# Attention in place and one unit deeper, all turned copies on ScalarE, query blocks in the order 0, 3, 2, 1

## The reference

```python
# first block, "nsa": for each of 4 query blocks of 128 tokens and each of 4 heads
p_c = masked_softmax(q . k_cmp, ...)        # 31 compressed keys
p_s = masked_softmax(q_rope . k_sel, ...)   # keys up to the query
p_w = masked_softmax(q_rope . k_win, ...)   # keys up to the query
prob = softmax(q_mem . mem_k)               # 256 memory keys
# second block, "dsa": for each of 4 query blocks, 16 heads
rel = relu(einsum('bqhd,bsd->bhqs', qib, k_idx))        # 8 index heads
score = einsum('bqh,bhqs->bqs', wb, rel)                # causal
_, sel = lax.top_k(score, topk)                         # topk = 128
p = softmax(q . k at the selected, valid keys)
o = p @ v at the same keys
```

## Time and profile before

| | |
|---|---|
| three executions | 2140.89, 2128.39, 2145.9 us (median 2140.89) |
| profiled execution, device time | 2129.25 us |
| its span in the profile | 2127.3 us |
| `stage_nsa`, attention part | about 459 to 609 us |
| `stage_dsa`, index items | about 772 to 798.5 us |
| `stage_dsa`, attention part | about 798.5 to 966 us |
| `stage_dsa`, output turned and copied | about 967 to 972.4 us |

### The profile page before, as it was taken

The page is one execution under the profiler, slowest core; times in us unless marked ns, Lnnn a source line. Parts: engine busy times, 40 slices in busy tenths (PEclk is TensorE's granted clock), DMA queues, the critical chain, the costliest instruction groups (busy, mean ns, idle before and its releaser), DMA issues. The chain is left out here.

```text
span 2127.3 us, 31283 instructions
## 1 busy us (share of the span) xinstructions
PE 1922.6 (90%) x12332; PEld 1519.9 (71%) x12332; DVE 973.7 (46%) x1686; ACT 824.1 (39%) x1304; POOL 259.9 (12%) x209
## 2 busy tenths in 40 slices
PE   5999389879978889998799999989999889999997
PEld 4887189745547646667688888868888768888885
DVE  2343835473354588834333333345555443333233
ACT  4223244433223443323444442246565244344322
POOL 3000223110003150000200000022222030000000
PEclk9999579865569995558799999989999899999998
DMA  4321100000002110002122333322222113322331
GB/s 169 98 90 45 38 5 3 29 17 1 1 22 84 50 31 1 1 1 60 60 91 96 99 94 100 94 72 88 73 71 60 41 60 99 99 94 94 99 99 50
DMA packets 37762, 131.66 MB, mean 62 GB/s; under 512 B 4817, under 2 KB 5137, under 8 KB 37393
## 3 DMA queue, kind: packets, MB, share of 16 engines
q1 hardware_dynamic: 36784, 127.91, 19.0%
q10 hardware_dynamic: 864, 2.17, 0.3%
HBM read 127.17 MB, written 2.10 MB: 61 GB/s over the span
## 5 line engine op out<-in xcount | busy, mean ns | idle before, releaser
L138 DVE TENSOR_TENSOR big_parts<-ring,big_parts 128x1024 fp32r<-128x1024 f32 x164 | 205.1, 1252 | 526.8 <-ACT big_parts L133 526.8
L156 PE MATMUL bank<-h_parts,big_parts 128*128 128x512 f32 x960 | 381.9, 398 | 26.0 <-POOL y_parts L1402 17.6
L157 PE MATMUL bank<-y_parts,big_parts 128*128 128x512 f32 x960 | 377.8, 394 | 0.0
L158 PE MATMUL bank<-h_parts,big_parts 128*128 128x512 f32 x960 | 377.5, 393 | 0.0
L133 ACT ACTIVATE big_parts<-ring 128x1024 fp32r<-128x1024 f32 x164 | 173.7, 1061 | 289.2 <-PE bank L158 289.0
L156 PEld LDWEIGHTS bank<-h_parts,big_parts 128*128 128x128 f32 x960 | 182.9, 191 | 67.3 <-issue 28.3
L158 PEld LDWEIGHTS bank<-h_parts,big_parts 128*128 128x128 f32 x960 | 182.7, 190 | 38.5
L157 PEld LDWEIGHTS bank<-y_parts,big_parts 128*128 128x128 f32 x960 | 183.1, 191 | 37.3
L157 PE MATMUL bank<-y_parts,work_parts 128*128 128x512 f32 x456 | 181.4, 398 | 0.0
L138 DVE TENSOR_TENSOR work_parts<-ring,work_parts 128x1024 fp32r<-128x1024 f32 x65 | 79.3, 1223 | 168.0 <-ACT work_parts L133 168.0
L995 ACT ACTIVATE work<-work 128x256 f32<-128x256 f32 (+4 forms) x128 | 67.1, 525 | 209.7 <-DVE work L1013 209.6
(11 more groups left out here) (399 smaller groups left out, 3121.3 us busy)
## 6 DMA issues: line engine op xcount, KB each, us to landing
ring<-in_wstream SPq DMA_DIRECT2D x229, 512.0 KB, 3.5
x<-in_xt SPq DMA_DIRECT2D x4, 512.0 KB, 7.9
out_t<-x SPq DMA_DIRECT2D x8, 256.0 KB, 2.0
work<-in_memt ACTq DMA_DIRECT2D x1, 1024.0 KB, 15.4
work<-in_cw SPq DMA_DIRECT2D x1, 1024.0 KB, 5.1
cst<-in_cst ACTq DMA_DIRECT2D x1, 704.0 KB, 7.9
cos<-in_reset SPq DMA_DIRECT2D x2, 256.0 KB, 2.6
big<-work SPq DMA_DIRECT2D x4, 128.0 KB, 4.0
```

What stands on the lines that cost most here:

```text
L138: dve.tensor_tensor(self.parts[:, self.place_of(n), 1, :, :], self.ring[:, n % RING, :, :], self.parts[:, self.place_of(n), 0, :, :].bitca ...
L156: pe.matmul(out, w[0], x[0], start=start, stop=False, skip_group_check=True)
L157: pe.matmul(out, w[0], x[1], start=False, stop=False, skip_group_check=True)
L158: return pe.matmul(out, w[1], x[0], start=False, stop=stop, skip_group_check=True)
```

## The change

Four things change in `Attend` and one in `stage_dsa`. R writes its masked scores straight into the weights buffer and X works in it in place; the buffers are five `e` and four `t` in place of three `s`, three `e` and three `t`. T comes three turns after S and V four (they were two and three). All copies C stand on ScalarE. The code is split into one function for an engine's turn. In `stage_dsa` the blocks come in the order 0, 3, 2, 1, for the index items (3, 2, 1), for the units and for the picks. A function `warm` is added that can put extra matmuls ahead of T, but no caller gives it any (`fill` is empty), so it issues nothing.

```diff
-    ROLL = 3
...
+    WEIGHTS, TURNS = 5, 4
+    TURN, SUM = 3, 4
...
-    def tensor(self, pe):
+    def tensor_turn(self, pe, n):
...
-            if 0 <= n - 2 < len(units):
-                i = n - 2
-                u, b = units[i], c.bank[self.TURNED[i % 3]]
-                self.wait_weights(pe, i)
-                if i >= 3:
-                    self.wait_copied(pe, i - 3)
+        if 0 <= n - self.TURN < len(units):
+            i = n - self.TURN
+            b = c.bank[self.TURNED[i % 3]]
+            if i >= 3:
+                pe.wait_ge(self.copied, i - 2)
+            warm(c, pe, b, self.fill.get(i, 0))
+            self.wait_weights(pe, i)
...
+    def scalar_turn(self, act, n):
         units = self.units
-        for n in range(len(units) + 2):
-            if n < len(units):
-                u = units[n]
-                act.wait_ge(self.maxed, n + 1)
-                if n >= 3:
-                    act.wait_ge(self.turned, n - 2)
-                act.activation(self.e[n % 3][:, 0:u.keys], self.s[n % 3][:, 0:u.keys], ACT.Exp, bias=self.low[:, n:n + 1],
-                               scale=-1.0, accum_out=self.den[:, n:n + 1]).then_inc(self.exped, 1)
-            if 0 <= n - 2 < len(units) and self.by_act(n - 2):
-                self.turn_copy(act, n - 2)
+        if n < len(units):
+            act.wait_ge(self.maxed, n + 1)
+            e = self.weights(n)
+            act.activation(e, e, ACT.Exp, bias=self.low[:, n:n + 1], scale=-1.0, accum_out=self.den[:, n:n + 1])\
+               .then_inc(self.exped, 1)
+        if 0 <= n - self.TURN < len(units):
+            i = n - self.TURN
+            act.wait_ge(self.turned, i + 1)
+            if i >= self.TURNS:
+                act.wait_ge(self.summed, i - self.TURNS + 1)
+            parts = units[i].parts
+            w, cols = parts[0][1], len(parts) * P
+            act.activation(self.t[i % self.TURNS][0:w, 0:cols], self.c.bank[self.TURNED[i % 3]][0:w, 0:cols], ACT.Copy)\
+               .then_inc(self.copied, 1)
...
+    def vector_turn(self, dve, n):
...
+            if n >= self.WEIGHTS:
+                dve.wait_ge(self.turned, n - self.WEIGHTS + 1)
+            dve.tensor_tensor_reduce(self.weights(n), self.c.bank[self.SCORES[n % 3]][:, 0:u.keys], u.mask, -self.scale, 3e38,
+                                     ALU.add, ALU.min, self.low[:, n:n + 1]).then_inc(self.maxed, 1)
...
-    items = [(q, h) for q in range(1, QT) for h in range(IH)]
+    late = (3, 2, 1)
+    items = [(q, h) for q in late for h in range(IH)]
...
-    for q in range(QT):
+    for q in (0, *late):
...
-                q = n // (TOPK // 8) + 1
-                if q < QT:
+                if n < len(late) * TOPK // 8:
+                    q = late[n // (TOPK // 8)]
```

More of the change, by code:

```diff
@@ L158, in product, with warm @@
     return pe.matmul(out, w[1], x[0], start=False, stop=stop, skip_group_check=True)
+def warm(c, pe, bank, n):
+    for _ in range(n):
+        pe.matmul(bank[:, :], con(c, "ident"), c.cst[:, 0:4, :], start=True, stop=True)
 class TileParts:
@@ L974, in turn_copy @@
[L974 to L985, removed]
@@ new lines, in tensor_turn @@
+        if n < len(units):
+            u = units[n]
+            if n >= 3:
+                pe.wait_ge(self.maxed, n - 2)
+            scores = c.bank[self.SCORES[n % 3]][:, 0:u.keys]
+            if isinstance(u.q, tuple):
+                mm = product(pe, scores, u.q, u.k, True, True)
+            else:
+                mm = pe.matmul(scores, u.q, u.k, start=True, stop=True)
+            mm.then_inc(self.scored, 1)
+        if 0 <= n - self.TURN < len(units):
[5 more added lines that the diff above has]
+            self.wait_weights(pe, i)
+            for j, w in units[i].parts:
+                mm = pe.transpose(b[0:w, j:j + P], self.weights(i)[:, j:j + w], con(c, "ident"))
+            mm.then_inc(self.turned, 1)
@@ new lines, in tensor_turn @@
+        if 0 <= n - self.SUM < len(units):
+            i = n - self.SUM
+            u, g, at = units[i], i // self.group, i % self.group * HD
+            pe.wait_ge(self.copied, i + 1)
+            if g >= 2 and at == 0:
+                pe.wait_ge(self.finished, g - 1)
+            out = c.bank[self.OUT[g % 2]]
+            for x, (j, w) in enumerate(u.parts):
+                for half in (0, HD):
+                    mm = pe.matmul(out[half:half + HD, at:at + HD], self.t[i % self.TURNS][0:w, j + half:j + half + HD],
+                                   u.vals[x], start=x == 0, stop=x == len(u.parts) - 1, skip_group_check=True)
+            mm.then_inc(self.summed, 1)
@@ L1034, with turns @@
+    def turns(self):
+        return range(len(self.units) + self.SUM)
 NC = (T - 32) // 16 + 1
@@ L1214, in _ @@
         def _(pe):
-            at.tensor(pe)
+            for n in at.turns():
+                at.tensor_turn(pe, n)
             for q in range(QT):
@@ L1224, in _ @@
         def _(act):
-            at.scalar(act)
+            for n in at.turns():
+                at.scalar_turn(act, n)
             act.wait_ge(o_sem, 2)
@@ L1971, in pick @@
                         ch.link(dve.tensor_scalar(v["mask"][:, q, 0:w], s, -2e38, -1e30, ALU.is_gt, ALU.mult))
-            at.vector(dve, pick)
+            for n in at.turns():
+                pick(n)
+                at.vector_turn(dve, n)
             for q in range(QT):
```

108 lines of the change are left out of this document (34 added, 74 removed).

## The result

| | before | changed |
|---|---|---|
| median of 20 executions | 2135.38 us | 2143.48 us |
| lowest to highest | 2128.39 to 2145.9 | 2135.49 to 2149.42 |
| profiled execution, device time | 2129.25 | 2135.49 |
| its span | 2127.3 | 2133.3 |

The ratio is 1.0034, with a 95% interval of 1.002 to 1.0048: slower by 0.2 to 0.5%, within the 1% that the prediction set as its bound for no change. The forecast was 2143, in a range of 2122 to 2157. By the two medians the change costs 8.1 us, by the ratio 7.3; the forecast had +4.1.

What follows compares the result with a forecast made beforehand. TensorE's work at 1.2 GHz was taken as the bound. Terms -0.6 - 0.5 + 1.0 + 0.5 + 0.1 + 0.9 + 2.7 gave +4.1 us; with 2140 against the mean and 2145 against the median, 2143 us was set, range 2122 to 2157.

Steps and rivals of the forecast that it cites:

- V with idle time put down to ScalarE: Sign of a wrong forecast: in the changed profile T or V shows idle time put down to ScalarE.
- What bounds the kernel: Attention parts: TensorE's work at 1.2 GHz sets their end, full in blocks 3, 2 and 1, 3.68 us a turn in block 3.
- Three times nothing: Where TensorE is full: copies leaving VectorE, copies given to ScalarE and buffers in place are worth nothing.
- Start and end of the nsa part: Nsa part: S of unit 3 fills the idle start, -0.6 us; one more T and V moves into the end, -0.5.
- Index items: Dsa stage's index part: the order gives nothing, the wider first matmul delays the head, +1.0 us, between 0 and +2.5.
- First pick: Ahead of R of unit 0 in the dsa stage: pick of 512 keys in place of 256, +0.5 us.
- Block 0 of the dsa stage: VectorE takes over the pace at 1.72 us a turn; 23.2 us to turn 16 against 23.1 before, +0.1 us.
- turn 16 starts when R of unit 13 is done: Dsa block 0: S of unit n waits for R of n - 3, so turn 16 starts 23.2 us behind R of unit 0.
- ScalarE's queue is too tight: Rival: V waits for a copy behind S, R, X, C; chain above 1.8 us costs +28 us, about 2175; chance 0.05.
- One more T and V: Dsa stage when turn 16 starts: one more T and one more V of 128 keys still to do, +0.9 us.
- Output: Dsa stage's output: transposes stay at 1.2 GHz, 7.4 us for 32, 8.2 against 5.6 in all, +2.7 us.
- The rival of the clock: Rival: the clock rises inside the dsa part, about -50 us from the middle of block 3, about 2092; chance 0.05.

Runs made afterwards that it cites:

- e6: Changed kernel with the copies C of even units given back to VectorE; ratio to before 1.0019, block 0 27.37 us.
- e5: Changed kernel with the old depth, T two turns and V three turns after S; ratio to before 1.0022, block 0 26.21 us.
- e2: Changed kernel with the dsa stage's blocks in the old order 0, 1, 2, 3; ratio to before 0.9973, median 2132.15 us.
- e4: Changed kernel with four extra 512-column matmuls ahead of T of unit 16 in the dsa stage; ratio to before 0.981, median 2093.47 us.
- e9: Changed kernel with old block order 0, 1, 2, 3 and four extra matmuls ahead of T of unit 16; ratio to before 1.0011, median 2140.23 us.
- e3: Kernel before with only the dsa stage's block order changed to 0, 3, 2, 1; ratio to before 1.0047, median 2144.52 us.
- e1: Changed kernel with copy C of unit n - 3 ahead of X of unit n on ScalarE; ratio to before 1.0026, block 0 24.48 us.
- e7: Changed kernel with copy C of unit n - 2 ahead of X of unit n on ScalarE; ratio to before 1.0013, median 2136.48 us.
- e8: e7 plus four extra matmuls at unit 16 of the dsa stage and at units 20, 36, 52 of nsa; ratio to before 0.9626, median 2059.1 us.
- e10: e9 without the picks (max and match_replace), so keys are not selected; ratio to before 0.9746, blocks behind block 0 91.95 us.

## Why the prediction was right, and the step that failed

The direction held, and so did the size in the rough: +4.1 us forecast, +6.3 in the pieces of the two profiles, +7.3 by the ratio. That 2143 met the measured 2143.48 is luck. The forecast set it by a base of about 2139, taken from four executions, and the median of 20 before is 2135.38: a base 3.5 us too high made up for a change 3 to 4 us too small. The ends that the prediction names for its terms add up to -0.5 and +6.7; the +7 is there, the -2 is not. One of its own signs of being wrong was seen: V with idle time put down to ScalarE (2.85 us, ahead of V of unit 0).

- *What bounds the kernel.* Right. TensorE is full at 0.50 in blocks 3, 2 and 1, and the turn of block 3 is 3.67 us. "Three times nothing" held for the copies where TensorE is full: e6 and the changed kernel have 143.34 both. The depth there is worth the 0.82 us of e5; the buffers in place weren't tried apart. For the copies it failed in block 0 alone, on the side of a gain, by 1.2 us (e6).
- *Start and end of the nsa part.* -1.1 predicted, -1.6 in the two profiles. But the same code took 147.34 us in the changed kernel, 147.90 in e2, 148.55 in e4, 147.22 in e9 and 147.44 in e10, and the old code 148.95 before and 148.63 in e3. One execution doesn't resolve the term; the two means (147.69 and 148.79) differ by 1.1, as predicted. That the clock rises at the end was right.
- *Index items.* +1.0 predicted, +1.06 measured, and in the pieces predicted: the order gives nothing, the head costs. VectorE's 24 items take 24.98 us from the first start to the last end in both kernels. From the first matmul to the first item it is 773.88 - 771.17 = 2.71 us now and was 773.52 - 771.87 = 1.65. Beside GpSimd a 512-column item took 8.14 / 5 = 1.63 us (1.65 predicted), one of 256 free of it 4.02 / 7 = 0.57 (0.58). The changed kernel's rows in order of time:

```profile
771.17 4.60 PE L1899 MATMUL bank<-big 128*128 128x512 f32 x5 [2.67 <-PEq L90]
...
773.88 0.49 DVE L1944 TENSOR_SCALAR work<-work 128x512 f32<-128x512 f32 x1 [3.93 <-ACT work L1920]
...
778.29 8.14 DVE L1947 SCALAR_TENSOR_TENSOR work<-work 128x512 f32<-128x512 f32 x5 [0.25 <-ACT work L1920]
...
794.84 4.02 DVE L1947 SCALAR_TENSOR_TENSOR work<-work 128x256 f32<-128x256 f32 x7
```

and the same place before, which the earlier trace rows begins a little later:

```profile
771.87 3.75 PE L1909 MATMUL bank<-big 128*128 128x256 f32 x8 [2.67 <-PEq L90]
...
773.52 0.35 DVE L1952 TENSOR_SCALAR work<-work 128x256 f32<-128x256 f32 x1 [2.86 <-ACT work L1929]
```

- *First pick.* +0.5 predicted, +0.53 measured.
- *Block 0 of the dsa stage.* **This is the step that failed:** "turn 16 starts when R of unit 13 is done", +0.1, measured +3.14. The pace was right. But S is not the only thing that follows VectorE. V of unit n - 4 in TensorE's turn n waits for C of n - 4, behind X of n - 1, behind R of n - 1, and S of turn n + 1 stands behind that V. S of unit 16 so waits for R of unit 14 and then for X, C and V of 0.4, 0.26 and 0.4 us with their hops, in place of R of unit 13 alone. By the rows: 14 x 1.73 + 0.83 for a group end, and 808.29 - 806.84 = 1.45 from R of unit 3 to the next S, less 0.29 for R of unit 0 itself, give 26.2, and 26.20 was measured. With C ahead of one X (e1) the same chain hangs on R of unit 13: 13 x 1.73 + 0.83 + 1.45 - 0.29 = 24.5, measured 24.48. With C ahead of two (e7) only the wait of S for R of unit 13 is left, 13 x 1.73 + 0.83 = 23.3, measured 23.36. This is the mechanism of the rival "ScalarE's queue is too tight". The prediction had the chain and weighed it against 1.8 us of TensorE's own work in a turn, as though R of a unit always came early; where VectorE sets the pace R comes last, and the chain costs one turn of VectorE and its own length behind R. In the other blocks it costs nothing, so that the rival's +28 us for 80 turns did not come.
- *One more T and V.* +0.9 predicted for what remains to be done, +1.47 measured: mis-sized. With e5's depth it is 0.82 less, so the deeper part was sized right and the 0.6 us beside it belong to the order (e3 has +0.73 in the old code). They are the clock again: before, it was up for the last 0.8 us of this piece, and in the new order it wasn't; a transpose takes 0.116 us with the clock up and 0.23 at 0.50, so these 0.8 us of work are worth about as much again. The row of before:

```profile
965.20:966.00 0.80, 0.78 (x26) 0.64 (x22) 0.00 (x0) 0.04 (x1) 0.00 (x0) 1.00 0.00 0
```

- *Output.* +2.7 predicted, +1.75 measured: mis-sized. The clock stayed down behind the S-less end, as forecast, but not through the whole output: it rose in the last quarter of the transposes (0.50 to 977.90, 1.00 behind 977.95), so that the 32 transposes took 6.42 us and not 7.4. When it rises isn't fixed: the piece takes 7.48 to 8.17 us in the other runs with this order and no extra matmuls, and 6.43 in every run where the clock is up at its start.

```profile
972.35 6.42 PE L1909 MATMUL bank<-cst,h 128*128 128x128 f32 x32 [0.86 <-DVE h L1878]
```

- *The rival of the clock* had the right size (-50 us; e4 saves 49.55 in the stage) and did not come by itself. Its reason against was right: 102 us of blocks 3 and 2 at 0.50.

The Trainium skill (TensorE: Matmul & The Clock Gate, Part 1) says that activity releases the throttle and that a steadily busy engine stays at full clock. Here the trace disagrees with a busy time as the measure: 55.00 of 55.00 us at 0.50. Its Part 4 says that PE-mode transposes do not count as busy in the same way. The output's row speaks against it: TensorE did nothing but 32 transposes from 972.35 on, and the clock rose from 0.50 to 1.00 after 5.6 us of them.

## What to carry to other kernels

Where one engine sets the pace of a ring, look at each wait of the other engines for what stands ahead of it in the queue of the engine waited for: here the exponentials of later units ahead of an older copy cost 2.8 us once, the first of them a full turn of the pacemaker (1.72 us), and a deeper pipeline didn't help (26.21 and 26.20 us). TensorE was full at 0.50, and every rearrangement around it moved the dsa stage by 9 us at most; four extra matmuls moved it by 50. So where TensorE is full at 0.50, try first what a few large matmuls at the start of the stretch do to its clock. Then look in the trace for where it falls again: at holes that another engine makes (e9), for which it may help to put the longest TensorE work beside the heaviest work of that engine, and at stretches of small units, which can lose the clock with TensorE never idle (e8).

## What the runs showed of the hardware

The granted clock has two levels at which the same sequence of matmuls goes on. Without help it stayed at 0.50 for the 102 us of blocks 3 and 2, at 100% busy; lifted by 6 us of extra matmuls it stayed at 1.00 for the 78 us shown (e4), with 96.9% busy. It fell again in e9 behind holes of 1.15 and 0.23 us. In e10, with the same TensorE program and no such holes, it stayed, so the units of that stretch alone don't take it away; the picks that e10 leaves out do, most likely by the holes. In e4 TensorE also stood idle, for 0.95 us of the first 30, and for 0.55 at most at a time in the whole stretch, and the clock stayed. In e8 it fell twice with no hole at all, where T and V were of 31 keys, so holes are not the only way to lose it. How large a hole or how light a stretch it takes, the runs don't settle; none varied either in steps.
